# A hand-ordered transformer kernel on one core: key products placed behind the next group's first projection, and small norms placed between attention steps

## The chip, the cores and the metric

The kernel runs on one core of one Trainium2 chip. The metric is the device time of one execution in microseconds (us), taken as the median of several runs.

The engines are named as in the profile: PE is TensorE (matrix products), PEld its weight loads, DVE is VectorE, ACT is ScalarE, POOL is GpSimd and SP is SyncE. Each engine runs its own list of instructions in the order of the program and waits at semaphores for the others.

## The reference, cut to what matters

Two transformer blocks run one after the other on 512 tokens of width 1024, all in float32. The first block is a mixer (a short convolution and differential attention), a cross-attention, and a layer of product-key experts. The second block is a mixer of three parts, a cross-attention and a feed-forward layer with a short convolution.

The change touches two places. The first is how the experts are chosen:

```
q = (hc @ w_pq).reshape(PEER_CHUNK, PEER_HEADS, 2, PEER_DK_HALF)
sc = jnp.einsum('thcd,chnd->thcn', q, sub_keys)        # 128 keys a half
vals, idx = lax.top_k(sc, PEER_TOPK)
cand = vals[:, :, 0, :, None] + vals[:, :, 1, None, :]
top_s, top_c = lax.top_k(cand..., PEER_TOPK)           # 16 experts a head and token
ue, ve = peer_u[experts], peer_v[experts]              # gathered rows
act = gelu(einsum('td,thkd->thk', hc, ue)); out = einsum('thk,thkd->td', g * act, ve)
```

The second is the second block's mixer. Beside the sparse attention (`nsa`) it has a gated part and a convolution part, each with a layer norm, and all three are normed before the output projection:

```
v = layer_norm(v, ln_g, ln_b); mixed = einsum("gts,bcsgd->bctgd", w_s * causal, v) + b_s; y_gmlp = u * mixed
h = causal_depthwise_conv(a * sigmoid(gt), dw_w, dw_b);  y_conv = silu(layer_norm(h, ln_g, ln_b))
y = concat([rms_norm(y_nsa), rms_norm(y_gmlp), rms_norm(y_conv)]);  x = x + y @ w_out
```

## The kernel before, in words

**Halves and tiles.** The 512 tokens are worked on in two halves, `h` = 0 and 1, of 256 tokens, and each half is two tiles of 128 tokens, so that there are four tiles `t`. A projection is cut in chunks. SP loads the chunk's 512 KB of weights into one of six buffers (`RING`), PE multiplies (`proj_T` at L876/L877, `proj_tok` at L896/L897), and the result is copied or combined out of PSUM (`out_T`, `out_tok`) by ACT or DVE.

**One written order.** The class `Plan` writes one list of steps, and each engine follows its own part of that list, in order. Three generators are woven: `work` (the projections and attention of half 1 of block one, then block two of half 0), `choices` (the two rounds of top-16 on DVE, the picking of indices, the softmax of gates) and `peers` (the experts). Each generator has a clock that its steps' costs advance, and the one with the lowest clock goes next. A step that must come after another generator's work yields "wait" until that work is in the list. After the weave, the second block of half 1 (`second(1, False)`) comes alone, and beside it runs `late_down`, the feed-forward output projection of half 0, of which `beside(n)` puts n chunks (L1120; the trace shows a chunk as four instructions of 128x512) between other steps.

**Experts.** For each of 512 experts (128 to a tile) POOL gathers 128 rows of 8 KB (L2125) into one of eight slots, DVE takes a dot product (L1908), ACT applies gelu (L1409), scales it by the gate (L1413, L1416) and, where PE is to add, builds a diagonal matrix (L1421). The sum is made by DVE (L1888) or by PE (L1144/L1145). A slot is free when its sum is done. POOL waits for that.

**Key products.** `scores(h)` runs four groups `c` of four projection chunks `m`. With `lean`, all results leave PSUM on ACT (L1242) into `QH[:, c % 2]`. After a group's fourth chunk is copied out, PE multiplies the group by its keys for both tiles (`scores` on PE, L993), and ACT copies the products out (L1397). DVE's `top` (L1816, L1819, L1824) waits for that copy. `gates` on ACT (L1403) is an exponential, and `gate_sum` on DVE (L1872) waits for it. In half 1 the norm of the second memory follows group 1, and its eight transposes (`trans`, L864/L865, copied out at L1222) follow group 3's products.

**The second block's mixer.** `second(h)` runs twenty steps of `nsa`, a software pipeline over 16 units: PE makes logits (L1088), DVE adds the mask and takes the maximum (L1685), ACT takes exponentials (L1482), DVE weighs them (L1954 to L1969), PE transposes (L1053, L1055), ACT and DVE copy these out (L1500, L2002), and PE multiplies by the values (L1067, L1073). Up to step 15, DVE does four taps of the 31-tap convolution in each step (L1994). After the twenty steps come, in this order:

- `gmlp`: two layer norms on DVE (L2007 to L2023) with a square root on ACT in each (`root`, L1196), PE's gated products (L1096), and DVE's product with u (L2035);
- `conv_out`: PE transposes the convolution (L1105, L1106), two more layer norms, and a silu on ACT (L1519);
- `y_norm`: for each of three parts of `Y`, two squares on ACT (L1191), mean and reciprocal on DVE (L1561, L1563), a square root on ACT (L1196), and then six scalings on DVE (L2054);
- in half 1, the last six chunks of `late_down`, then the transposes of `y` (L864/L865) and the output projection.

**Banks.** The eight PSUM banks are handed out in turn. During the weave six are, since the sums of the experts hold two. A bank is given again when its reader has copied it out.

Of the kernel before, what the change touches and what calls it, by code (L numbers as in the profile page):

```python
# [10 lines left out]
ALU = mybir.AluOpType  # L11
# [91 lines left out]
class Plan:  # L103
# [167 lines left out]
    def scores(self, h, lean):  # L271
        if h == 1:
            self.lent_from = self.last_in.get(7)
        held = None
        for c in range(4):
            for m in range(4):
                k = self.next_ring()
                yield 0, "chunk", "pq", 4 * c + m, k
                if held:
                    yield (0, "out_T") + held  # L280
                yield 3.4, "proj_T", "pq", h, c, m, k
                held = ("pq", h, c, m, lean)
# [4 lines left out]
            if h == 1 and c == 1:  # L287
                yield 0, "mark", ("mem", 2)
                yield from self.norm_steps(("mem", 2), lean)
                self.norming = False  # L290
            if h == 1 and c == 3:
                for i in range(8):
                    yield 0, "trans", ("mem", 2), i, lean
            self.reached.add(("sc", h, c))
# [171 lines left out]
def program(nc, I, out):  # L466
    ctx = ExitStack()
    with ctx:
# [138 lines left out]
        SQ = WKF[:, 0:1024]  # L607

        at = Values()
        ps_of = {}  # L610
# [198 lines left out]
        def tensor_program(e, w):  # L809
# [280 lines left out]
            def gmlp(h):  # L1090
                for c in range(2):
                    ps = bank("gm", h, c)
                    w.wait_ge(*at["ln1", h, c])
                    w.wait_ge(*at["ws"])
                    for g in range(4):
                        mm = e.matmul(ps[:, 64 * g:64 * g + 64], WS[:, g, :], ZG[h][:, c, 256 + 64 * g:320 + 64 * g],  # L1096
                                      start=True, stop=True)
                    mm.then_inc(pe.sem, pe("mm", "gm", h, c))

            def conv_out(h):  # L1100
                for c in range(2):
                    ps = bank("ct", h, c)
                    for m in range(2):
                        w.wait_ge(*at["cv", h, m, 30])
                    e.transpose(ps[:, 0:128], CV[h][:, 0, c * 128:(c + 1) * 128], ident[:, :])  # L1105
                    e.transpose(ps[:, 128:256], CV[h][:, 1, c * 128:(c + 1) * 128], ident[:, :]).then_inc(  # L1106
                        pe.sem, pe("mm", "ct", h, c))
# [71 lines left out]
        def scalar_program(e, w):  # L1179
# [330 lines left out]
            def gmlp(h):  # L1510
                for c in range(2):
                    root(("ln1", h, c), small[:, 407 + 8 * c:408 + 8 * c])

            def conv_out(h):
                for c in range(2):
                    root(("ln2", h, c), small[:, 423 + 8 * c:424 + 8 * c])
                    w.wait_ge(*at["ln2", h, c])
                    d = Y[h][:, c, 768:1024]
                    e.activation(d, d, ACT.Silu).then_inc(act.sem, act("ycv", h, c))  # L1519

            def y_norm(h):
                w.wait_ge(*at["ev", "nv", h, 15])
                w.wait_ge(*at["ev", "gm", h, 1])
                w.wait_ge(*at["ycv", h, 1])
                for q in ENGINES:
                    w.wait_ge(*at["mark", ("y", h), q])
                for j, (a, b) in enumerate(((0, 512), (512, 768), (768, 1024))):
                    squares(("y", h, j), lambda i: Y[h][:, i, a:b], 2, b - a, 448 + 2 * j)
                    root(("y", h, j), small[:, 448 + 2 * j:450 + 2 * j])
# [14 lines left out]
            def hank_in():  # L1544
# [8 lines left out]
                    "nsa": nsa, "gmlp": gmlp, "conv_out": conv_out, "y_norm": y_norm, "mark": marks(act, "act")})  # L1553

        def vector_program(e, w):
# [469 lines left out]
            def gmlp(h):  # L2025
                for c in range(2):
                    v = ZG[h][:, c, 256:512]
                    layer_norm(("ln1", h, c), v, v, "ln1g", "ln1b", 400 + 8 * c, ("ev", "zg", h, 0, 1), ("ln1", h, c))
                for c in range(2):
                    ps = banks[ps_of["gm", h, c]]  # L2030
                    w.wait_ge(*at["mm", "gm", h, c])
                    w.wait_ge(*at["cols"])
                    for g in range(4):
                        sig = ("ev", "gm", h, c) if g == 3 else ("gmp", h, c, g)
                        e.scalar_tensor_tensor(out=Y[h][:, c, 512 + 64 * g:576 + 64 * g], in0=ps[:, 64 * g:64 * g + 64],  # L2035
                                               scalar=col("bs", g), in1=ZG[h][:, c, 64 * g:64 * g + 64], op0=ALU.add,
                                               op1=ALU.mult).then_inc(dve.sem, dve(*sig))

            def conv_out(h):
                for c in range(2):  # L2040
                    layer_norm(("ln2", h, c), banks[ps_of["ct", h, c]][:, 0:256], Y[h][:, c, 768:1024], "ln2g", "ln2b", 416 + 8 * c,
                               ("mm", "ct", h, c), ("ln2", h, c), ("ev", "ct", h, c))

            def y_norm(h):
                parts = ((0, 512), (512, 768), (768, 1024))
                for j, (a, b) in enumerate(parts):
                    inverse(("y", h, j), small[:, 448 + 2 * j:450 + 2 * j], b - a, 1e-6)
                for j in range(3):
                    w.wait_ge(*at["rstd", ("y", h, j)])
                for i in range(2):  # L2050
                    for j, (a, b) in enumerate(parts):
# [19 lines left out]
            def prepare_lambda():  # L2071
                w.wait_ge(*at["rows"])
                for j, (a, b) in enumerate((("lq1", "lk1"), ("lq2", "lk2"))):
# [12 lines left out]
                    "conv_out": conv_out, "y_norm": y_norm, "down": down, "mark": marks(dve, "dve")})  # L2086
# [180 lines left out]
```

## Time and profile before

| what | value |
|---|---|
| median of 3 runs | 2953.93 us (2953.39 to 2955.98) |
| the profiled execution: its time | 2952.47 us |
| its span in the trace | 2950.7 us |
| PE / DVE / ACT / POOL busy | 85% / 60% / 38% / 23% of the span |
| granted PE clock, mean | 0.916 of full speed |
| mean rate of HBM | 284 GB/s |

The profile is of one execution. An engine's share of the span is an average over stages with different limits, so the rows below are read by stretch. The stages of the span, in the order in which the change meets them: the key products of half 0 end near 608 us; those of half 1 run from 1331 to 1434 us; the second block's attention of half 0 runs from about 1672 to 1838 us and its tail to 1879 us; experts go on to 2329 us; the attention of half 1 runs from 2420 to 2553 us and its tail to about 2580 us.

### The profile page before, as it was taken

To read this page: it belongs to the slowest core of one execution; us is meant where nothing else is said; L and a number is where in the kernel's file an instruction comes from. 1 tells how busy PE (TensorE), PEld (TensorE's weight loads), DVE (VectorE), ACT (ScalarE), POOL (GpSimd) and SP (SyncE) were. 2 spreads that over 40 slices of the span, in tenths; PEclk is the share of its full clock that TensorE was granted. 3 is DMA by queue.
4 is the path that set the end of the run, shared out by engine and by line. 5 is a ranking of instruction groups with operands and counts; after the bars stand their busy time and mean duration, and the time that the engine had idled before them with its cause. 6 is when DMAs were issued, how large, how long until landed. Compare 5 with 4: busy or idle time off the path is not lost.

```text
span 2950.7 us, 29550 instructions
## 1 busy us (share of the span) xinstructions
PE 2497.3 (85%) x10118; PEld 1749.2 (59%) x10118; DVE 1760.5 (60%) x4222; ACT 1131.8 (38%) x2759; POOL 681.8 (23%) x566
## 2 busy tenths in 40 slices
PE   8999998889987769779869688587985799888998
PEld 7786665767764337537627544264762476555883
DVE  2101311588697778676879998878998416412430
ACT  2101311242534754454333587464554324412210
POOL 0000000122244334331123445344324101000000
PEclk9999999899998879999989588799997989999999
DMA  6545344689999999999789999899999744432553
GB/s 203 175 153 165 93 143 134 254 302 365 377 400 419 380 405 393 419 368 360 263 337 385 399 372 373 325 419 419 417 418 416 270 155 122 135 130 86 150 154 117
DMA packets 159814, 838.64 MB, mean 284 GB/s; under 512 B 17272, under 2 KB 20744, under 8 KB 93872
## 3 DMA queue, kind: packets, MB, share of 16 engines
q0 software_dynamic: 73728, 536.90, 45.5%
q1 hardware_dynamic: 81312, 287.75, 28.4%
q10 hardware_dynamic: 4624, 12.11, 1.1%
q8 instruction: 80, 1.31, 0.2%
q14 instruction: 70, 0.57, 0.1%
HBM read 828.27 MB, written 8.41 MB: 284 GB/s over the span
## 4 chain that ended last, share of the span: by engine, by line
PE 54%; DVE 18%; ACT 12%; DMA 10%; issue 5%; POOL 1%; DVEq 0%; ACTq 0%; SPq 0%
PE ps L876 25%; DMA BIG<-in_uv,BIG 8%; PE ps L896 5%; PE ps L1120 5%; PE ps L897 5%; DVE X L1888 5%; DVE BIG L1908 5%; PE ps L877 3%; ACT L1409 2%; PE ps L1144 2%; PE ps L1145 2%; DMA BIG<-head_scratch 1%; PE ps L1088 1%; ACT WK L1191 1%; DVE BIG L1819 1%
## 5 line engine op out<-in xcount | busy, mean ns | idle before, releaser
L2125 POOL DMA_INDIRECT BIG<-in_uv,BIG x512 | 639.2, 1249 | 1659.6 <-DVE BIG L1865 556.9
L876 PE MATMUL ps<-BIG,RING 128*128 128x256 f32 x3472 | 807.5, 385 | 16.1 <-DMA RING<-in_w_cq 4.9
L876 PEld LDWEIGHTS ps<-BIG,RING 128*128 128x128 f32 x3472 | 670.0, 194 | 135.3 <-issue 26.4
L1908 DVE CUSTOM_DVE_ANT_0 BIG<-BIG 128x1024 f32<-128x1024 f32 x512 | 620.2, 1220 | 71.0 <-DMA BIG<-in_uv,BIG 68.0
L1888 DVE SCALAR_TENSOR_TENSOR X<-BIG,small,X 128x1024 f32<-128x1024 f32 x333 | 427.6, 1284 | 100.5 <-ACT small L1413 100.2
L1409 ACT ACTIVATE small<-small 128x1 f32<-128x1 f32 x512 | 102.4, 200 | 609.4 <-DVE small L1908 606.3
L876 PE MATMUL ps<-WK,RING 128*128 128x256 f32 x1232 | 289.2, 387 | 24.6 <-DVE BIG L1667 22.6
L876 PEld LDWEIGHTS ps<-WK,RING 128*128 128x128 f32 x1232 | 236.5, 193 | 65.4 <-DVE BIG L1667 30.7
L896 PE MATMUL ps<-RING,BIG 128*128 128x512 f32 (+1 forms) x448 | 225.7, 585 | 7.1 <-DVE BIG L1646 4.4
L897 PE MATMUL ps<-RING,BIG 128*128 128x512 f32 (+1 forms) x448 | 224.1, 582 | 0.0
L1242 ACT ACTIVATE BIG<-ps 128x256 f32<-128x256 f32 (+2 forms) x143 | 56.4, 397 | 402.5 <-PE ps L877 343.0
L1605 DVE TENSOR_SCALAR BIG<-ps 128x256 f32<-128x256 f32 (+2 forms) x37 | 16.8, 454 | 252.1 <-PE ps L877 207.7
L864 PE MATMUL ps<-ident,BIG 128*128 128x128 f32 x128 | 49.6, 396 | 135.2 <-ACT BIG L1213 77.0
L1120 PE MATMUL ps<-RING,BIG 128*128 128x512 f32 x352 | 161.5, 612 | 1.5 <-DVE X L1898 1.5
L1144 PE MATMUL ps<-BIG 128*128 128x512 f32 x178 | 106.3, 682 | 59.6 <-ACT BIG L1421 59.5
L1409 ACT ACT_TABLE_LOAD x119 | 152.7, 1283 | 2.7 <-issue 0.6
L877 PE MATMUL ps<-BIG,RING 128*128 128x256 f32 x496 | 147.5, 379 | 0.0
L896 PEld LDWEIGHTS ps<-RING,BIG 128*128 128x128 f32 x448 | 85.2, 192 | 104.7 <-issue 93.0
L1598 DVE TENSOR_TENSOR X<-ps,X 128x512 f32<-128x512 f32 x40 | 27.4, 690 | 201.0 <-PE ps L897 125.1
L897 PEld LDWEIGHTS ps<-RING,BIG 128*128 128x128 f32 x448 | 85.9, 192 | 102.5 <-issue 101.1
L1144 PE MATMUL ps<-BIG,DG 128*128 128x512 f32 x180 | 111.6, 706 | 34.9 <-ACT DG L1421 34.5
L1191 ACT ACTIVATE WK<-X 128x1024 f32<-128x1024 f32 x32 | 33.8, 1055 | 224.7 <-DVE X L1598 210.6
(255 smaller groups left out, 3143.0 us busy)
## 6 DMA issues: line engine op xcount, KB each, us to landing
RING<-in_w_up SPq DMA_DIRECT2D x88, 512.0 KB
RING<-in_w_down SPq DMA_DIRECT2D x66, 512.0 KB
RING<-in_w_pq SPq DMA_DIRECT2D x32, 512.0 KB
RING<-in_w_cc SPq DMA_DIRECT2D x16, 512.0 KB
RING<-in_w_cx SPq DMA_DIRECT2D x16, 512.0 KB
RING<-in_w_cb SPq DMA_DIRECT2D x16, 512.0 KB
RING<-in_w_cv SPq DMA_DIRECT2D x16, 512.0 KB
RING<-in_w_gc SPq DMA_DIRECT2D x16, 512.0 KB
```

What stands on the lines that cost most here:

```text
L876: e.matmul(ps[:, 0:256], W[:, j, :], src[:, j, 0:256], start=j == 0, stop=False)
L877: e.matmul(ps[:, 0:256], W[:, 7, :], src[:, 7, 0:256], start=False, stop=True).then_inc(pe.sem, pe("mm", site, h, c, m))
L896: e.matmul(ps[:, 0:n], src[:, 2 * j, t * 128:(t + 1) * 128], W[:, 0, :], start=j == 0, stop=False)
L897: mm = e.matmul(ps[:, 0:n], src[:, 2 * j + 1, t * 128:(t + 1) * 128], W[:, 1, :], start=False, stop=j == 3)
L1120: mm = e.matmul(ps[:, :], AF[h][:, f, t * 128:(t + 1) * 128], W[:, hh * 512:(hh + 1) * 512], start=f == 0, stop=f == 21)
L1144: e.matmul(banks[6][:, :], d, v[:, 0:512], start=first, stop=last)
L1145: e.matmul(banks[7][:, :], d, v[:, 512:1024], start=first, stop=last).then_inc(pacc.sem, pacc("sum", k))
L1191: e.activation(SQ[:, 0:width], src(i), ACT.Square, accum_out=small[:, o + i:o + i + 1]).then_inc(act.sem, act("sq", key, i))
L1409: e.activation(a, dots[:, k % 8:k % 8 + 1], ACT.Gelu).then_inc(act.sem, act("gelu", k))
L1888: e.scalar_tensor_tensor(out=X[:, t, :], in0=slot[slot_of[k]][:, 1024:2048], scalar=acts[:, k % 8:k % 8 + 1], in1=X[:, t, :], op0=ALU.mult ...
L1908: e.tensor_tensor_reduce(out=u, in0=HF[:, t % 2, :], in1=u, scale=1.0, scalar=0.0, op0=ALU.mult, op1=ALU.add, accum_out=dots[:, k % 8:k % ...
L2125: e.indirect_dma_start(out=slot[i], out_offset=None, in_=I["uv"], in_offset=bass.IndirectOffsetOnAxis(ap=IDX[:, t, c:c + 1], axis=0)).then ...
```

## The change

**Key products.** A group's last copy out and its products are held back until the first chunk of the next group has been multiplied. Three exceptions stay where they were: group 0 of half 0, and group 3 of both halves, come right behind their own group. In half 1, the second memory's norm goes along with group 1, and its eight transposes come before group 3's products, not behind them.

**Norms.** The functions `gmlp` and `conv_out` are split by the tile index `c`, `gmlp` gets its layer norm as a step of its own (`gmlp_norm`), and these stand behind the attention steps 1 and 2 (norm), 4 and 5 (gated product), and 16 and 17 (convolution's transposes, layer norm and silu). The squares of the gated part and of the convolution part of `Y` stand behind the steps 18 and 19. Of `y_norm` there remain behind the attention: the squares of the attention part, all means and reciprocals (`y_inv`), all three square roots (`y_root`), and the scalings (`y_scale`). In the weave, the three first of these have a cost of 2.6 each, where `gmlp` and `conv_out` had 2.0 each. Those squares write their unused output to `JUNK`, a place of its own. The instructions that the program writes are those of before; none is added or left out. The loads of ACT's function tables are put in when the kernel is built, wherever the function changes.

```
     def scores(self, h, lean):
+        def lists(c):
+            if h == 1 and c == 3:
+                for i in range(8):
+                    yield 0, "trans", ("mem", 2), i, lean
+            for t in range(2):
+                yield 0.9, "scores", h, c, t, lean
+            if h == 1 and c == 1:
+                yield 0, "mark", ("mem", 2)
+                yield from self.norm_steps(("mem", 2), lean)
+                self.norming = False
+            self.reached.add(("sc", h, c))
...
                 yield 3.4, "proj_T", "pq", h, c, m, k
                 held = ("pq", h, c, m, lean)
-            yield (0, "out_T") + held
-            held = None
-            for t in range(2):
-                yield 0.9, "scores", h, c, t, lean
...
+                if m == 0 and c and (h or c > 1):
+                    yield from lists(c - 1)
+            if c == 3 or (h == 0 and c == 0):
+                yield (0, "out_T") + held
+                held = None
+                yield from lists(c)
...
+        gap = 2.6 if lean else 0
+        other = {1: ("gmlp_norm", h, 0), 2: ("gmlp_norm", h, 1), 4: ("gmlp", h, 0), 5: ("gmlp", h, 1),
+                 16: ("conv_out", h, 0), 17: ("conv_out", h, 1), 18: ("y_sq", h, 1), 19: ("y_sq", h, 2)}
         for step in self.phase(True, ((8.0, "nsa", h, i) for i in range(20))):
             self.norming = lean and step[3] >= 18
             yield step
+            if step[3] in other:
+                yield (0,) + other[step[3]]
             yield from beside(1 + step[3] % 2)
-        yield 2.0, "gmlp", h
-        yield 2.0, "conv_out", h
         yield 0, "mark", ("y", h)
-        yield 0, "y_norm", h
+        yield gap, "y_sq", h, 0
+        yield gap, "y_inv", h
+        yield gap, "y_root", h
+        yield 0, "y_scale", h
         yield from beside(7)
...
+            def y_sq(h, j):
+                a, b = Y_PARTS[j]
+                w.wait_ge(*at[(("ev", "nv", h, 15), ("ev", "gm", h, 1), ("ycv", h, 1))[j]])
+                if j == 0:
+                    for q in ENGINES:
+                        w.wait_ge(*at["mark", ("y", h), q])
+                for i in range(2):
+                    own()
+                    e.activation(SQ[:, 0:512] if j == 0 else JUNK, Y[h][:, i, a:b], ACT.Square,
+                                 accum_out=small[:, 448 + 2 * j + i:449 + 2 * j + i]).then_inc(act.sem, act("sq", ("y", h, j), i))
```

## Rows read from the trace of the kernel before

**Rows 1.** Busy time by stretch; columns: stretch, length, PE, PEld, DVE, ACT, POOL busy (instructions), PE clock, DMA share, GB/s.

```profile
560.00:622.00 62.00, 40.14 (x171) 31.51 (x169) 53.52 (x183) 24.97 (x56) 17.88 (x17) 0.84 0.94 368
...
1437.00:1518.00 81.00, 80.41 (x247) 48.22 (x248) 61.54 (x195) 25.94 (x70) 20.08 (x19) 0.98 0.85 317
...
1680.00:1836.00 156.00, 130.69 (x420) 70.69 (x420) 144.27 (x477) 123.47 (x356) 76.73 (x56) 0.85 0.96 377
1836.00:1882.00 46.00, 12.05 (x52) 9.68 (x51) 33.82 (x75) 25.11 (x57) 12.32 (x11) 0.59 0.71 282
...
1912.00:2320.00 408.00, 311.31 (x1128) 218.71 (x1128) 341.91 (x557) 211.50 (x492) 153.14 (x128) 0.90 1.01 418
...
2422.00:2553.00 131.00, 130.96 (x591) 83.99 (x590) 73.64 (x353) 58.19 (x161) 23.02 (x16) 0.95 0.38 112
```

**Rows 2.** Timeline, one full-clock projection chunk to the next (start, length, what).

```profile
1337.28 3.19 PE L876 MATMUL ps<-BIG,RING 128*128 128x256 f32 x14
...
1340.73 3.18 PE L876 MATMUL ps<-BIG,RING 128*128 128x256 f32 x14
```

**Rows 3.** Timeline of half 0's group 2: PE, ACT and DVE (idle before it in brackets).

```profile
584.23 3.75 PE L993 MATMUL ps<-WK,BIG 128*128 128x128 f32 x16 [9.06 <-ACT BIG L1242]
...
588.02 0.60 ACT L1397 ACTIVATE BIG<-ps 128x512 f32<-128x512 f32 x1 [1.11 <-PE ps L993]
...
589.93 0.23 ACT L1403 ACTIVATE BIG<-BIG 128x32 f32<-128x32 f32 x1
...
590.19 0.19 DVE L1872 TENSOR_REDUCE small<-BIG 128x2 f32<-128x32 f32 x1 [4.82 <-ACT BIG L1403]
```

**Rows 4.** Timeline of half 1's groups 0, 2 and 3 on PE and DVE.

```profile
1352.79 0.49 DVE L1816 MAX8 BIG<-BIG 128x8 f32<-128x128 f32 x2 [8.60 <-ACT BIG L1397]
...
1406.11 3.75 PE L993 MATMUL ps<-WK,BIG 128*128 128x128 f32 x16 [7.44 <-ACT BIG L1242]
...
1410.36 0.19 DVE L1872 TENSOR_REDUCE small<-BIG 128x2 f32<-128x32 f32 x1 [2.69 <-ACT BIG L1403]
...
1437.60 4.95 PE L876 MATMUL ps<-BIG,RING 128*128 128x256 f32 x14 [1.95 <-ACT BIG L1222]
```

**Rows 5.** Timeline, half 0's tail: the first two norms, the transposes of y.

```profile
1848.12 0.42 DVE L2007 BATCH_NORM_STATS2 small<-BIG 128x6 f32<-128x256 f32 x1
...
1850.67 0.42 DVE L2007 BATCH_NORM_STATS2 small<-BIG 128x6 f32<-128x256 f32 x1
...
1875.42 0.45 PE L864 MATMUL ps<-ident,BIG 128*128 128x128 f32 x1 [19.25 <-DVE BIG L2054]
```

**Rows 6.** Who waited on DVE, 1848 to 1882 us (total, times, longest).

```profile
DVE small L1561 <- ACT WK L1191: 4.9, 3, 2.2
...
DVE BIG L2015 <- ACT small L1196: 1.9, 4, 1.1
DVE BIG L2035 <- PE ps L1096: 1.3, 1, 1.3
```

**Rows 7.** Timeline of DVE and ACT at half 0's attention step 16.

```profile
1818.17 1.20 DVE L1908 CUSTOM_DVE_ANT_0 BIG<-BIG 128x1024 f32<-128x1024 f32 x1
...
...
1820.77 1.28 ACT L1409 ACT_TABLE_LOAD   x1
1822.06 0.20 ACT L1409 ACTIVATE small<-small 128x1 f32<-128x1 f32 x1
```

**Rows 8.** Timeline of half 1's tail.

```profile
2556.09 1.14 PEld L1096 LDWEIGHTS ps<-BIG,WS 128*128 128x128 f32 x8 [0.39 <-DVE BIG L2023]
...
2558.64 1.10 PE L1096 MATMUL ps<-BIG,WS 128*128 128x64 f32 x8 [1.27 <-DVE BIG L2023]
...
2560.03 10.46 PE L1120 MATMUL ps<-RING,BIG 128*128 128x512 f32 x24
...
2575.85 0.45 PE L864 MATMUL ps<-ident,BIG 128*128 128x128 f32 x1 [5.36 <-DVE BIG L2054]
```

**Rows 9.** Who waited on DVE, 2405 to 2560 us.

```profile
DVE BIG L2002 <- PE ps L1055: 24.7, 13, 6.4
```

More of the change, by code:

```diff
@@ L607, in program @@
         SQ = WKF[:, 0:1024]
+        JUNK = at_(K0 + 4632, 256)
+        Y_PARTS = ((0, 512), (512, 768), (768, 1024))
         at = Values()
@@ L1088, in nsa, with gmlp, conv_out @@
                         e.matmul(ps[:, 0:nn], q, K, start=True, stop=True).then_inc(pe.sem, pe("mm", "nl", h, u, j))
[L1090 to L1107, printed above, removed]
+            def gmlp(h, c):
+                ps = bank("gm", h, c)
+                w.wait_ge(*at["ln1", h, c])
+                w.wait_ge(*at["ws"])
+                for g in range(4):
+                    mm = e.matmul(ps[:, 64 * g:64 * g + 64], WS[:, g, :], ZG[h][:, c, 256 + 64 * g:320 + 64 * g],
+                                  start=True, stop=True)
+                mm.then_inc(pe.sem, pe("mm", "gm", h, c))
+            def conv_out(h, c):
+                ps = bank("ct", h, c)
+                for m in range(2):
+                    w.wait_ge(*at["cv", h, m, 30])
+                e.transpose(ps[:, 0:128], CV[h][:, 0, c * 128:(c + 1) * 128], ident[:, :])
+                e.transpose(ps[:, 128:256], CV[h][:, 1, c * 128:(c + 1) * 128], ident[:, :]).then_inc(
+                    pe.sem, pe("mm", "ct", h, c))
             def down(h, f, k, tiles):
@@ L1508, in nsa, with gmlp_norm, conv_out, y_root @@
                         act.sem, act("ev", "nv", h, u))
[L1510 to L1528, printed above, removed]
+            def gmlp_norm(h, c):
+                root(("ln1", h, c), small[:, 407 + 8 * c:408 + 8 * c])
+            def conv_out(h, c):
+                root(("ln2", h, c), small[:, 423 + 8 * c:424 + 8 * c])
+                w.wait_ge(*at["ln2", h, c])
+                d = Y[h][:, c, 768:1024]
+                e.activation(d, d, ACT.Silu).then_inc(act.sem, act("ycv", h, c))
+            def y_sq(h, j):
[8 more added lines that the diff above has]
+                                 accum_out=small[:, 448 + 2 * j + i:449 + 2 * j + i]).then_inc(act.sem, act("sq", ("y", h, j), i))
+            def y_root(h):
+                for j in range(3):
                     root(("y", h, j), small[:, 448 + 2 * j:450 + 2 * j])
@@ L2023, in layer_norm @@
                 e.tensor_tensor(dst, dst, row(b, key[1]), ALU.add).then_inc(dve.sem, dve(*fin))
[L2025 to L2046, printed above, removed]
+            def gmlp_norm(h, c):
+                v = ZG[h][:, c, 256:512]
+                layer_norm(("ln1", h, c), v, v, "ln1g", "ln1b", 400 + 8 * c, ("ev", "zg", h, 0, 1), ("ln1", h, c))
@@ new lines, in gmlp @@
+            def gmlp(h, c):
+                ps = banks[ps_of["gm", h, c]]
+                w.wait_ge(*at["mm", "gm", h, c])
+                w.wait_ge(*at["cols"])
+                for g in range(4):
+                    sig = ("ev", "gm", h, c) if g == 3 else ("gmp", h, c, g)
+                    e.scalar_tensor_tensor(out=Y[h][:, c, 512 + 64 * g:576 + 64 * g], in0=ps[:, 64 * g:64 * g + 64],
+                                           scalar=col("bs", g), in1=ZG[h][:, c, 64 * g:64 * g + 64], op0=ALU.add,
+                                           op1=ALU.mult).then_inc(dve.sem, dve(*sig))
@@ L2050, in y_norm @@
                 for i in range(2):
-                    for j, (a, b) in enumerate(parts):
+                    for j, (a, b) in enumerate(Y_PARTS):
                         o = 448 + 2 * j + i
```

18 lines of the change are left out of this document (8 added, 10 removed).

## The prediction

> **What bounds the kernel now.** I read the page first: PE is busy for 85% of the span, but the chain that ended last is shared between PE, DVE, ACT and gathers, so no one engine is the bound and each place must be read by itself. I then read the busy time by stretch, the timelines of the places that the change touches, and who waited for whom there.
>
> Four kinds of stretch follow one another [rows 1]. Where half 0's key products run (560 to 622 us), DVE is busy for 53.52 of 62 us and PE for 40.14: DVE and its waits set the pace. From 1437 to 1518 us PE is busy for 80.41 of 81 us. From 1680 to 1836 us, half 0's attention beside the experts, DVE is busy for 144.27 of 156 us. From 1912 to 2320 us the DMA share is 1.01: the gathers are the bound, and projections of half 0 made sooner there end nothing sooner; only experts that have come further by 1912 do. From 2422 to 2553 us, half 1's attention, PE is busy for 130.96 of 131 us.
>
> All lists are written in one order, so a time saved where an engine sets the pace moves everything behind it forward, unless another bound has covered it.
>
> **Key products, half 0.** Groups 0 and 3 stay. Group 1 moves past one projection chunk, 3.45 us from start to start [rows 2]. DVE waits for its first gather then, and I cost this edit at nothing; without that cover it would be up to 3.45 us. Group 2 is the one that counts. Its products waited 9.06 us for a copy out that ACT made only after an expert's gelu, and began at 584.23. ACT copied both results out, the second at 588.02, and only then made the exponential (589.93), for which DVE's gate sum had waited 4.82 us at 590.19 [rows 3]. With the products one chunk later in the list, `gates` falls ahead of them (the products' 3.4 of clock against 0.9), so ACT makes its 1.28 us table load and 0.23 us exponential right behind the copy out, by about 585.7. DVE then needs group 2's first result. PE has the next chunk behind it already and can begin the products at 584.2 as before: half of 3.75 us and a 0.60 us copy give 586.8. Before, DVE reached that work at 590.19 and its three small instructions, 590.7. So 3.9 us are saved on DVE, which sets the pace. Bounds: nothing, and the idle time with the chunk gained, 4.82 us.
>
> **Key products, half 1.** Here group 0 moves too, and DVE stood idle for 8.60 us until 1352.79 for just that result [rows 4]. It comes at least 3.45 us later. An expert's dot product (1.20 us [rows 7]) or two will be listed ahead of it in that hole, so DVE lags by 1 to 3 us. At group 2, PE's 7.44 us of idle time holds the next chunk, and DVE's wait of 2.69 us for the exponential goes as in half 0. I count half of these 2.69 us, 1.3, as what is left after the lag. At group 3 the memory's transposes come first, so that their copies lie beside the products: the 1.95 us that the next projection waited go, and its first chunk, 4.95 us at 1437.60 because PE's clock had fallen in the pauses, should take the 3.19 us of [rows 2], 1.8 us less. These 3.7 us are saved on PE, which is full from there to 1518 [rows 1]. The exponential of `gates` comes behind the eight copies now, so DVE waits there somewhat longer; DVE has 19 us of idle time in the 81 that follow, which hide it. In all 5.0 us. Bounds: a loss of 1 us, if the lag of 3 stays and PE must wait for experts' gates; a gain of 7.2 us, 3.7 and the whole chunk of 3.45.
>
> **Norms, half 0.** Nothing is taken out; work moves from the tail into an attention in which DVE is nearly full. Each of four layer norms costs DVE 2.55 us (1848.12 to 1850.67 [rows 5]). What can be gained is idle time. In the tail DVE waited 4.9 us for squares, 1.9 us for roots and 1.3 us for PE [rows 6], 8.1 us in all. With the squares ahead and the rest beside experts these go. In exchange, DVE now stands at each root behind ACT's exponentials. Read at step 16: DVE ends the step's own work about 1818.2 and needs some 0.9 us up to the reciprocal, but ACT is free only at 1820.77 and then has a load of 1.28 us and a root of 0.20 us, 1822.25 [rows 7]: a wait of 3.1 us. Queued behind it on DVE are the dot products, and for these ACT's gelu, PE's sums and POOL's free slots. I take 3.1 us for this worst step and half, 1.5 us, for each of the three others, 7.7 us. Net: a gain of 0.4 us. Bounds: a gain of 8.1 us if the 12 us in which DVE is idle in 1680 to 1836 take these waits, and a loss of 8 us if they are twice as long. The moved matrix products, transposes and silus cost the same and lie where PE is no bound. POOL and SP issue nothing new; the output projection's weights are asked for behind the same chunks.
>
> ACT goes from one table to the next with 0.01 us between the load's end and the gelu (1820.77, 1.28, 1822.06) [rows 7]. The Trainium skill ("ScalarE: Activation LUTs", What ACT_TABLE_LOAD costs) states a drain of about 1.38 us beside each load, 2.66 us a switch, and advises to group functions by table, which speaks against roots between exponentials. By that rule each of the four waits would be 1.38 us longer and the sum 5.5 us higher, about 2943 us; by the row it stays. The trace shows the load's length as stated and no drain.
>
> **Norms, half 1.** PE is the bound, and it waited 0.39 and 1.27 us for the gated products and 5.36 us for the normed y, 7.0 us together [rows 8]. DVE waited 24.7 us at one place of the pipeline alone for PE [rows 9] and is busy 73.64 of 131 us, so four norms of 2.55 us, and a wait for PE's gated product at steps 4 and 5, are hidden by PE's attention and feed-forward chunks; without that cover it would be 10 us. What is late next is the y norm itself: it can begin when the last attention result is out, near 2553, and needs two squares, six small instructions, a load of 1.28 us, three roots of 0.20 us [rows 7] and six scalings; I estimate some 7 us, half of it the squares and scalings (eight passes over at most 512 elements, at about the 0.42 us of 256 elements in [rows 5]), so it is done near 2560. PE then still has its six chunks, 10.46 us [rows 8], so nothing is late. A gain of 7.0 us, bounds 5 and 7.3.
>
> **The sum.** -3.9 - 5.0 - 0.4 - 7.0 = -16.3 us. The profiled execution took 2952.47 us (span 2950.7), so 2936.2 us; it lies 1.5 us under the median of 2953.93, so the forecast for a median is 2937.6, rounded to 2938 us. The order in the weave shifts by an expert or so at each moved step, which I can't cost; I allow 4 us to either side.
>
> **The rivals.**
> 1. The key products bring nothing (chance 0.20). The lag of half 1's first top-16 and the later results eat what the chunk gives. For it: the 8.60 us hole ends exactly with that result. Against: the 4.82 us wait. The norms alone give 7.4 us: 2946.5 us.
> 2. Half 0's norms are hidden after all (0.13). DMA's share is 0.71 from 1836 to 1882 against 1.01 later, 14 us of gathering not done [rows 1]. If the moved norms fall into time in which DVE waits for gathers anyway, the 8.1 us are a full gain: 2930 us.
> 3. The change doesn't do what it says in half 1's tail (0.10): the y norm's chain is stretched by DVE's leftovers of step 17 or by bank order, so that PE still waits about 5 us, and half 0 loses 4 us: 2947 or, with rival 1 as well, 2953 us, no change.
> 4. Slower (0.07): half 0's attention takes the DVE work and the tail gives nothing back, because the gathers were the bound there too. Four norms at their work of 2.55, 1.7 us of gated products and four waits of 3.1 us make 24 us against 15.9 gained elsewhere: 2962 us. It decides against the change when the waits pass 2.5 us each and nothing is refunded. For it: the DMA share of 0.96 in the attention. Against: the 14 us of idle DMA.
>
> **How the numbers follow.** My forecast has a chance of 0.50, with a range of its own from 2932 to 2943. Eight times in ten I expect 2926 to 2952, which takes in rivals 1 and 2 and the better part of 3. A measurement here can tell about 0.2%, 5.9 us. Faster by more than that, under 2948: forecast, rivals 1 and 2, less their edges, 0.77. Within it: most of rival 3 and edges, 0.15. Slower: rival 4 and part of 3, 0.08.
>
> **What would show it.** Half 0's group 2: DVE's wait at L1872 of 4.82 us under 1 us. Half 1: the products of group 0 one chunk later, DVE's hole longer; at group 3 no 1.95 us wait ahead of the next projection and its first chunk near 3.2 us. Half 0: waits of DVE at L2015 of 1 to 3 us in steps 1, 2, 16 and 17, a DMA share above 0.71 after the attention, and about as many experts done at the same time. Half 1: no idle PE ahead of L1096, and L864 right behind the last L1120. The prediction is wrong if DVE's added waits in half 0 are far from 8 us, if experts' order shifts by more than one or two at a step, or if PE's clock falls in a stretch where it was full.

## The result and the profile after

The changed kernel took 2939.4 us in the median of 6 runs (2936.01 to 2945.88), beside 2954.82 us of the kernel before (6 runs). The ratio is 0.9949, 95% interval [0.9933, 0.9965]: 15.1 us less, where 16.3 us less had been forecast. In a second series beside the other experiments the ratio was 0.9955 [0.9943, 0.9967], 13.3 us less. Two of the 29 executions of the kernel before in that series took 3711 and 3816 us at a granted clock of 0.66 and 0.64, and no ratio counts them. The profiled execution took 2945.88 us, with a span of 2944.2 us. It is the slowest of its six, so I use the second series' traced execution as well (2936.95 us, span 2935.2); "the first trace" and "the second trace" of the changed kernel below are these two.

The kernel's line numbers have moved: PE's L864 is now L880, L876 L892, L993 L1009, L1096 L1111, L1120 L1134; ACT's L1196 is L1210, L1397 L1411, L1403 L1417; DVE's L1872 is L1889, L1908 L1925, L1888 L1905, L1898 L1915, L2015 L2032, L2054 L2071.

Busy time by stretch, the changed kernel (columns as in [rows 1]):

```profile
560.00:622.00 62.00, 43.52 (x194) 34.67 (x194) 54.70 (x186) 25.85 (x60) 20.88 (x19) 0.86 0.98 387
1437.00:1518.00 81.00, 76.48 (x240) 45.21 (x238) 67.89 (x206) 26.77 (x69) 23.27 (x20) 0.99 0.93 352
1680.00:1836.00 156.00, 120.28 (x386) 65.33 (x387) 140.42 (x468) 120.28 (x337) 68.06 (x49) 0.84 0.89 351
1836.00:1882.00 46.00, 16.78 (x76) 11.08 (x74) 40.17 (x80) 28.88 (x77) 23.61 (x17) 0.70 0.98 379
...
1912.00:2320.00 408.00, 311.62 (x1128) 220.72 (x1128) 343.73 (x557) 211.99 (x492) 152.59 (x127) 0.90 1.01 415
2422.00:2553.00 131.00, 128.81 (x581) 82.55 (x580) 83.19 (x386) 70.84 (x175) 23.03 (x16) 0.95 0.37 111
```

In half 0 the gathers lost 0.07 of the DMA time in the attention (156 us) and won 0.27 of it in the 46 us of the tail: 10.9 us against 12.4 us. That is the exchange of which the forecast spoke. From 1912 to 2320 us the DMA share is 1.01 as before.

Timeline of half 0's group 2 in the changed kernel, against [rows 3]:

```profile
587.28 3.76 PE L1009 MATMUL ps<-WK,BIG 128*128 128x128 f32 x16 [6.57 <-ACT BIG L1256]
591.16 0.58 ACT L1411 ACTIVATE BIG<-ps 128x512 f32<-128x512 f32 x1
591.75 1.28 ACT L1417 ACT_TABLE_LOAD   x1
593.05 0.23 ACT L1417 ACTIVATE BIG<-BIG 128x32 f32<-128x32 f32 x1
593.31 0.19 DVE L1889 TENSOR_REDUCE small<-BIG 128x2 f32<-128x32 f32 x1
```

DVE's gate sum has no wait in brackets any more (it was 4.82 us). The exponential stands between the two copies out, not ahead of the first as I had read the list. Two smaller waits of the gate sum behind it, which the prediction had not read, are gone as well. In the kernel before they were:

```profile
616.10 0.19 DVE L1872 TENSOR_REDUCE small<-BIG 128x2 f32<-128x32 f32 x1 [1.07 <-ACT BIG L1403]
...
643.29 0.19 DVE L1872 TENSOR_REDUCE small<-BIG 128x2 f32<-128x32 f32 x1 [1.93 <-ACT BIG L1403]
```

The three waits were 7.8 us together.

Half 1's group 3 on PE, against [rows 4]:

```profile
1430.57 0.27 PE L880 MATMUL ps<-ident,BIG 128*128 128x128 f32 x1
...
1432.32 1.14 PE L1009 MATMUL ps<-WK,BIG 128*128 128x128 f32 x8
1433.30 1.02 PE L1158 MATMUL ps<-BIG 128*128 128x512 f32 x2
...
1435.01 1.05 PE L1009 MATMUL ps<-WK,BIG 128*128 128x128 f32 x8
1435.90 3.19 PE L892 MATMUL ps<-BIG,RING 128*128 128x256 f32 x14
```

The next projection has no wait, and its first chunk takes 3.19 us where it took 4.95. PE's wait of 1.28 us among the transposes is gone too. In the kernel before it was:

```profile
1434.84 0.33 PE L864 MATMUL ps<-ident,BIG 128*128 128x128 f32 x1 [1.28 <-ACT BIG L1222]
```

Half 1's tail on PE, against [rows 8]:

```profile
2557.97 0.43 PE L1089 MATMUL ps<-BIG 31*128 31x64 f32 x2
2558.33 14.00 PE L1134 MATMUL ps<-RING,BIG 128*128 128x512 f32 x32
2572.17 0.27 PE L880 MATMUL ps<-ident,BIG 128*128 128x128 f32 x1
```

L880 comes right behind the last chunk. Its transposes take 0.27 us each and not 0.45. In the kernel before, PE had stood idle for 5.36 us, and the clock granted to the transposes behind that was 0.50 of full speed, the lower of the two levels (1.2 GHz):

```profile
2575.80:2580.00 4.20, 3.93 (x16) 3.00 (x16) 2.74 (x6) 2.00 (x5) 0.00 (x0) 0.50 0.00 0
```

In the changed kernel it was 1.00, the upper level (2.4 GHz), from 2572.2 to 2575 us.

The y norm itself was done later than forecast. The last attention result came at 2558.4 us and not near 2553, ACT's first squares of the attention part waited until 2562.07, and DVE's scalings ended at 2567.3 where the forecast had said "near 2560". PE's last chunk ended at 2572.3, so the norm stayed hidden, with some 5 us to spare.

Who waited on DVE from 1640 to 1885 us in the changed kernel (total, times, longest), against [rows 6]:

```profile
DVE X L1905 <- ACT small L1427: 6.5, 10, 2.1
DVE BIG L2032 <- ACT small L1210: 6.4, 4, 1.6
DVE BIG L2052 <- PE ps L1111: 3.7, 1, 3.7
```

The four waits for a root are 6.4 us together; 7.7 us had been forecast. Each of them is 1.60 us. The third, with what ACT did during it:

```profile
1838.19 1.28 ACT L1210 ACT_TABLE_LOAD   x1
1839.48 0.20 ACT L1210 ACTIVATE small<-small 128x1 f32<-128x1 f32 x1
...
1839.72 0.54 DVE L2032 TENSOR_SCALAR BIG<-ps,small 128x256 f32<-128x256 f32 x1 [1.60 <-ACT small L1210]
```

All but some 0.1 us of the wait is the table load and the root. ACT had nothing else in hand: at none of the four did DVE stand behind exponentials, as the forecast had it.

The experts' progress shows how such a gain travels. Expert n is the n-th dot product of DVE (L1908 before, L1925 after; first rows of each here), and the table gives its start less that of the kernel before, in us. A plus is a lag, a minus a lead. A run's own offset at expert 0 is chance and may be taken off the whole column. One trace is one execution: five kernels whose list of steps is that of the kernel before up to the 144th expert lie there 0.1 to 3.7 us behind it with their offset taken off.

```profile
562.97 1.23 DVE L1908 CUSTOM_DVE_ANT_0 BIG<-BIG 128x1024 f32<-128x1024 f32 x1 [1.69 <-DMA BIG<-in_uv,BIG]
...
645.24 1.22 DVE L1908 CUSTOM_DVE_ANT_0 BIG<-BIG 128x1024 f32<-128x1024 f32 x1
```

```profile
565.33 1.23 DVE L1925 CUSTOM_DVE_ANT_0 BIG<-BIG 128x1024 f32<-128x1024 f32 x1 [4.67 <-DMA BIG<-in_uv,BIG]
...
640.78 1.22 DVE L1925 CUSTOM_DVE_ANT_0 BIG<-BIG 128x1024 f32<-128x1024 f32 x1
```

| expert (before at) | changed | changed, 2nd | order set back | half 0's keys alone | half 1's keys alone | all but half 0's keys | changed, sums on DVE |
|---|---|---|---|---|---|---|---|
| 0 (563.0) | +2.4 | +0.9 | -0.2 | +1.8 | +2.8 | +0.9 | -0.2 |
| 16 (645.2) | -4.5 | -5.9 | -7.0 | -5.1 | +2.8 | +1.0 | -7.0 |
| 32 (715.3) | -0.7 | -2.3 | -3.4 | -1.3 | +2.8 | +1.0 | -3.3 |
| 144 (1075.1) | +10.9 | +8.0 | +1.7 | +3.5 | +4.9 | +3.9 | +7.7 |
| 208 (1294.2) | +4.6 | +0.7 | +2.9 | -5.0 | +5.8 | +4.2 | +1.5 |
| 256 (1522.5) | -5.2 | -10.2 | -4.7 | +3.0 | -3.4 | -5.1 | -13.8 |
| 352 (1819.3) | +12.1 | +6.9 | +9.9 | +4.6 | -1.6 | +11.6 | +6.0 |
| 368 (1885.0) | -5.2 | -10.4 | -7.3 | +3.9 | -1.9 | -5.6 | -11.3 |
| 511 (2322.8) | -2.3 | -8.4 | -5.7 | +5.6 | +0.3 | -2.5 | -9.4 |

### The profile page after: what moved, and what is told of

Its sections match the earlier page's. It is cut to its first block, busy times and chain, and to the rows that moved or that the text cites. A ratio compares the mean times of both kernels' runs of the same rounds, so it can differ in the third digit from the quotient of the medians.

```text
span 2944.2 us, 29556 instructions
## 1 busy us (share of the span) xinstructions
PE 2499.7 (85%) x10118; PEld 1751.4 (59%) x10118; DVE 1760.1 (60%) x4222; ACT 1134.4 (39%) x2762; POOL 676.5 (23%) x566
## 4 chain that ended last, share of the span: by engine, by line
PE 57%; DVE 18%; ACT 11%; DMA 10%; issue 4%; POOL 0%; ACTq 0%; DVEq 0%; SPq 0%
PE ps L892 26%; DMA BIG<-in_uv,BIG 7%; PE ps L912 6%; PE ps L913 6%; PE ps L1134 5%; DVE BIG L1925 5%; DVE X L1905 4%; PE ps L893 4%; PE ps L1158 2%; PE ps L1159 2%; ACT L1423 2%; DMA BIG<-head_scratch 2%; DVE BIG L1836 1%; DVE BIG L1833 1%; PE ps L1104 1%
## 5 line engine op out<-in xcount | busy, mean ns | idle before, releaser
L892 PE MATMUL ps<-BIG,RING 128*128 128x256 f32 x3472 | 808.1, 385 | 13.8 <-DMA RING<-in_w_cq 4.9
L892 PEld LDWEIGHTS ps<-BIG,RING 128*128 128x128 f32 x3472 | 670.4, 194 | 133.7 <-issue 28.6
L1925 DVE CUSTOM_DVE_ANT_0 BIG<-BIG 128x1024 f32<-128x1024 f32 x512 | 619.4, 1218 | 73.0 <-DMA BIG<-in_uv,BIG 70.3
L1905 DVE SCALAR_TENSOR_TENSOR X<-BIG,small,X 128x1024 f32<-128x1024 f32 x333 | 426.9, 1282 | 108.7 <-ACT small L1427 106.7
L892 PE MATMUL ps<-WK,RING 128*128 128x256 f32 x1232 | 290.8, 389 | 21.7 <-DVE BIG L1684 19.9
L892 PEld LDWEIGHTS ps<-WK,RING 128*128 128x128 f32 x1232 | 238.6, 195 | 62.4 <-DVE BIG L1684 27.0
L912 PE MATMUL ps<-RING,BIG 128*128 128x512 f32 (+1 forms) x448 | 223.0, 579 | 5.1 <-DVE BIG L1663 2.4
L1134 PE MATMUL ps<-RING,BIG 128*128 128x512 f32 x352 | 161.9, 614 | 1.5 <-DVE X L1915 1.5
L1158 PE MATMUL ps<-BIG,DG 128*128 128x512 f32 x180 | 110.2, 698 | 61.3 <-ACT DG L1435 61.2
L880 PE MATMUL ps<-ident,BIG 128*128 128x128 f32 x128 | 48.0, 387 | 131.2 <-ACT BIG L1227 76.1
L912 PEld LDWEIGHTS ps<-RING,BIG 128*128 128x128 f32 x448 | 84.4, 190 | 102.1 <-issue 92.8
L1158 PE MATMUL ps<-BIG 128*128 128x512 f32 x178 | 109.2, 699 | 34.2 <-ACT BIG L1435 34.1
```

What stands on the lines that cost most here:

```text
L892: e.matmul(ps[:, 0:256], W[:, j, :], src[:, j, 0:256], start=j == 0, stop=False)
L912: e.matmul(ps[:, 0:n], src[:, 2 * j, t * 128:(t + 1) * 128], W[:, 0, :], start=j == 0, stop=False)
L1134: mm = e.matmul(ps[:, :], AF[h][:, f, t * 128:(t + 1) * 128], W[:, hh * 512:(hh + 1) * 512], start=f == 0, stop=f == 21)
L1158: e.matmul(banks[6][:, :], d, v[:, 0:512], start=first, stop=last)
L1905: e.scalar_tensor_tensor(out=X[:, t, :], in0=slot[slot_of[k]][:, 1024:2048], scalar=acts[:, k % 8:k % 8 + 1], in1=X[:, t, :], op0=ALU.mult ...
L1925: e.tensor_tensor_reduce(out=u, in0=HF[:, t % 2, :], in1=u, scale=1.0, scalar=0.0, op0=ALU.mult, op1=ALU.add, accum_out=dots[:, k % 8:k % ...
```

## The experiments

All ratios are to the kernel before on the same chip, and 0.001 is 2.95 us; kernels of different series are compared by these ratios, with both intervals. Parts that were "not moved" are written as in the kernel before.

**The two halves of the change, and a repetition.** The first kernel leaves the norms behind the attention (`gmlp_all`, `conv_all` and `y_norm` are the old steps, both tiles or all three parts at once):

```
         for step in self.phase(True, ((8.0, "nsa", h, i) for i in range(20))):
...
-            if step[3] in other:
-                yield (0,) + other[step[3]]
...
+        yield 2.0, "gmlp_all", h
+        yield 2.0, "conv_all", h
         yield 0, "mark", ("y", h)
-        yield gap, "y_sq", h, 0
-        yield gap, "y_inv", h
-        yield gap, "y_root", h
-        yield 0, "y_scale", h
+        yield 0, "y_norm", h
```

> Only the placing of the key products is changed; the norms stay behind the attention. My theory: a gain of 3.9 us in half 0 (group 2's exponential no longer behind the products) and 5.0 us in half 1 (group 3's transposes ahead of its products, one projection chunk inside PE's wait), so 8.9 us less than the kernel before, a ratio near 0.997. Rival 1, the key products bring nothing: 0 us, ratio 1.000. A third reading, that the traced run of the changed kernel suggests: the experts were up to 10.9 us behind between 1026 and 1140 us in it; if this comes from the new order of steps and not from that one execution, it is here again in the trace.

Measured: 0.9978 [0.9969, 0.9988], 6.5 us less. Rival 1 (the key products bring nothing) falls. The lag at the 144th expert was there again (+7.8 us), so it isn't the chance of one execution alone.

The second leaves the key products where they were (the loop of `scores` as before):

```
+                yield (0, "out_T") + held
+                held = None
+                for t in range(2):
+                    yield 0.9, "scores", h, c, t, lean
...
-                if m == 0 and c and (h or c > 1):
-                    yield from lists(c - 1)
```

> Only the norms are moved, in both halves; the key products stay. My theory: a gain of 0.4 us in half 0 and 7.0 us in half 1, 7.4 us in all, a ratio near 0.9975. If half 0's waits at the roots are not given back in the tail, slower than that by up to 8 us, so no gain; if they are hidden entirely, 15 us faster.

Measured: 0.9975 [0.9962, 0.9988], 7.4 us less, as forecast.

The third moves the norms in half 1 alone:

```
-            if step[3] in other:
+            if h == 1 and step[3] in other:
```

> Only the norms of half 1 are moved. My theory: 7.0 us less than the kernel before, a ratio near 0.9976, by the three waits of PE in the tail (0.39, 1.27 and 5.36 us) alone; the trace of the changed kernel shows 1.9 us of warm instead of cold transposes on top and some 2 us of new waits of PE in the attention. Rival 3, no gain in the tail: 0 us. The difference to the run in which both halves are moved is half 0's part: 0.4 us by my theory, 8 us either way by its bounds.

Measured: 0.9978 [0.9969, 0.9987], 6.5 us less. Half 0's norms are the difference to the kernel above, 0.9 us with an uncertainty of some 5 us: neither a gain of 8 us nor a loss of 8 us.

The fourth is the changed kernel again.

> The changed kernel itself once more, beside the others on one chip. The ratio should be near the 0.995 measured. If the experts' lag of 10.9 us near 1080 us belongs to the order of the steps, its new trace shows it again; if it was that one execution, it does not, and the span is shorter than 2944 us by several us.

Measured: 0.9955 [0.9943, 0.9967]; the lag was there (+8.0), and the span was 9.0 us shorter all the same.

**The key products by half, and the changed kernel without half 0's norms.** Half 0 alone has the new placing for h = 0 only, half 1 alone for h = 1 only (the loop of before under a condition on h).

> Only half 0's key products are placed anew (groups 1 and 2 one projection chunk later). My prediction's term: 3.9 us faster than the kernel before. The traces so far say otherwise: the experts are 7 us ahead at the 16th (645 us), 2 us ahead at the 64th to 112th, and 8 us behind at the 144th, because the shifted clock makes DVE meet the sum in another place of the differential attention's steps (9 us more of waiting for the scaled gate between 960 and 1090 us). By that: 1 us slower to 2 us faster, ratio 0.9995 to 1.0005, with the lag at the 144th expert in the trace.

Measured: 1.0022 [1.0011, 1.0033], 6.5 us more. Both theories missed it. On its own this part makes the kernel slower. The lead of the first 16 experts is there (-5.1 us). The lag that I expected at the 144th is not: +3.5 us, of which +1.8 is the offset, although the list of steps is the changed kernel's, step for step, up to the 220th expert. What the trace shows is later: 2.3 us ahead at the 255th expert, 3.0 us behind at the 256th. Between these two DVE stood at the total of tile 1, behind a sum that PE had behind chunks of the value projection (DVE's waits, 1460 to 1530 us, this kernel; then the kernel before):

```profile
DVE X L1964 <- PE ps L1195: 12.3, 1, 12.3
```

```profile
DVE X L1898 <- PE ps L1145: 1.2, 1, 1.2
```

In this kernel PE sums 11 of the last 16 experts of tile 1, among them the last, and in the kernel before ten, the last one by DVE. PE is full here from 1460 to 1520 us:

```profile
1460.00:1520.00 60.00, 60.00 (x173) 32.67 (x172) 40.13 (x128) 19.95 (x53) 16.31 (x15) 1.00 0.94 354
```

> Only half 1's key products are placed anew (all groups, and group 3's transposes first). My prediction's term: 5.0 us faster. If half 0's placing is worth nothing in the end, this one carries all of the 6.5 us that both gave (ratio 0.9978), and the trace shows no lag at the 144th expert. Rival: both are needed, and this one alone gives 3 us or less.

Measured: 0.9982 [0.9972, 0.9993], 5.3 us less; 5.0 had been the term. At the 144th expert, up to which its list is that of the kernel before, it stands at +4.9 against +2.8 at expert 0.

> The changed kernel, but half 0's norms stay behind its attention. My theory: half 0's norms are worth 0.4 us, so this is as fast as the changed kernel (ratio 0.9955). If half 0's move gave a gain of 8 us, this is 8 us slower than the changed kernel; if it cost one, it is faster: 2930 us.

Measured: 0.995 [0.9937, 0.9963], within the noise the same as the changed kernel. Half 0's norms are worth nothing that can be measured here either.

**Is the lag at the 144th expert worth time?** In half 1's differential attention each step lasts 9.0 on the work's clock and an expert 3.1, so three experts fall between two steps, and one of three is summed by DVE. So the same order comes back step after step. In the kernel before, from step 6 to 14, the expert that DVE sums is the second of the three and its sum comes last: three dot products of DVE stand between the step's own work and the sum. In the changed kernel, from step 3 to 12, that expert is the first, and only two dot products stand ahead of its sum, where DVE waits longer for the gate that ACT scales.

```
-        yield 0, "mark", ("da", h)
+        yield -2.5 * h, "mark", ("da", h)
```

> The changed kernel with the clock of the work generator set back by 2.5 at the start of half 1's differential attention, so that from step 5 to 14 the summed expert comes in the middle of three and the sum last, as in the kernel before (there from step 6 to 14; in the changed kernel only from step 14). No instruction is added. If the order of these steps makes the lag, the experts are some 8 to 10 us earlier at the 144th than in the changed kernel. In the time: a gain of up to 8 us if nothing behind it sets the pace, and 0 us if it is the lag that the kernel makes up by the 208th expert anyway; I expect 2 us faster than the changed kernel, ratio 0.995.

Measured: 0.9965 [0.9952, 0.9979]. DVE's wait for the scaled gate from 960 to 1090 us (total, times, longest) in the changed kernel, then in this one:

```profile
DVE X L1905 <- ACT small L1427: 37.8, 14, 6.0
```

```profile
DVE X L1905 <- ACT small L1427: 29.8, 13, 6.2
```

The 144th expert is at +1.7 instead of +10.9 and +8.0. Seven traces have the changed kernel's order in this stretch. With their offsets taken off, six of them lag by 6.2 to 8.6 us, with waits of 36.9 to 37.8 us, and one does not, that of half 0's keys alone (1.7 us):

```profile
DVE X L1954 <- ACT small L1463: 30.9, 14, 5.8
```

The kernel before and the five with its order wait 27.2 to 30.8 us. So the order makes the lag in most executions and not in every one; what decides was not found. And the kernel is not faster without it: the changed one makes the lag up by the 224th expert (-1.1 us), where half 1's key products on PE are waited for anyway. The total of tile 1 too had only 1.2 us of wait here, and that brought nothing visible either.

**The end of tile 1.** Here the last eight experts of tile 1 are summed by DVE, first with half 0's key products alone, then in the changed kernel:

```
-                    if n % 3 if self.light else n % 2:
+                    if (n % 3 if self.light else n % 2) and (t != 1 or c < 120):
```

> Half 0's key products alone, as in the run that was slower (1.0022), and the sums of the last eight experts of tile 1 on DVE, none of them on PE. In that slower run DVE waited 12.3 us at the total of tile 1 for a sum that PE had behind eight chunks of the value projection. My theory: this wait is what made it slower; without it the kernel is 3 to 6 us faster than that run, ratio 0.9998 to 1.001. Rival: PE is full there and sets the pace itself, then only the PE time of some five sums (1.7 us each) goes, and the ratio stays at 1.0015 or above.

Measured: 0.9997 [0.9988, 1.0006], 7.4 us less than the run at 1.0022 (by the two intervals 3 to 12 us less): the slowness is gone. Here six sums went from PE to DVE. The total is not waited for any more, and the kernel stands at the 256th expert at -0.6 us, 3.5 us ahead of the kernel before when the offset of +2.9 is taken off.

> The changed kernel with the same edit: the last eight experts of tile 1 are summed by DVE. It waited 8.6 to 10.8 us at that total in the two traces of the changed kernel, against 1.2 us before. By the theory of the wait: 3 to 6 us faster than the changed kernel, ratio 0.993 to 0.994. If PE sets the pace: 2 us or less, ratio 0.9945 or above.

Measured: 0.9912 [0.9896, 0.9928], 26 us less than the kernel before and 11 to 13 us less than the changed one, by the intervals anything from 4 to 19 us. It is faster than both theories had it. Five sums went from a full PE to a DVE that waited (1437 to 1518 us, second trace of the changed kernel, then this one; the total of tile 1 in the first trace of the changed kernel, then here):

```profile
1437.00:1518.00 81.00, 74.81 (x225) 42.70 (x223) 68.16 (x216) 28.09 (x74) 22.67 (x20) 0.96 0.94 354
```

```profile
1437.00:1518.00 81.00, 68.72 (x212) 40.17 (x210) 79.06 (x231) 31.07 (x78) 25.50 (x22) 0.93 0.96 369
```

```profile
1513.59 1.29 DVE L1915 TENSOR_TENSOR X<-ps,X 128x512 f32<-128x512 f32 x2 [10.82 <-PE ps L1159]
```

```profile
1504.92 1.29 DVE L1915 TENSOR_TENSOR X<-ps,X 128x512 f32<-128x512 f32 x2
```

Five sums of 1.72 us each (two instructions of L1158 and two of L1159) are 8.6 us of PE, and PE is busy for 6.1 and 7.8 us less than in the two traces of the changed kernel. I had called "PE sets the pace" a rival worth 2 us or less, and that size was wrong: if PE is the bound, its 8.6 us are the gain. This edit takes away both the wait and PE's work; the kernel with the order set back had only the wait taken away and won nothing. That speaks for PE's work, but the two were not separated in one pair of kernels, and the trace does not show the gain. It is of the slowest of only four executions (2924.08 to 2936.06 us), and with 2936.06 us as long as the changed kernel's second trace (2936.95). With the offsets taken off it is 2.5 us ahead of that trace at the 256th expert and level with it at the 511th. Where the 11 to 13 us of the untraced executions come from is open.

**Group 3's transposes alone**, in the kernel before:

```
+                if h == 1 and c == 3:
+                    for i in range(8):
+                        yield 0, "trans", ("mem", 2), i, lean
                 for t in range(2):
                     yield 0.9, "scores", h, c, t, lean
```

> The kernel before with one thing changed: in half 1 the eight transposes of the second memory come before group 3's products. My prediction's term for this alone: 3.7 us faster (1.95 us of PE's wait and 1.8 us of cold first chunk), ratio 0.9987. If it is 0, half 1's 5 us come from the products placed one chunk later.

Measured: 0.9984 [0.9971, 0.9997], 4.7 us less. The lists of the two kernels differ in nothing but this, so it is the cleanest pair here. It accounts for most of the 5.3 us of half 1's key products, as far as intervals of some 4 us can tell.

**All but half 0's key products.**

> The changed kernel, but half 0's key products stay where they were in the kernel before. By my prediction's term it loses 3.9 us against the changed kernel (ratio 0.9965). By the runs of the key products so far (half 1 alone 0.9982, both 0.9978, half 0 alone 1.0022) half 0's placing is worth nothing here or less: ratio 0.9935 to 0.9955.

Measured: 0.9967 [0.9955, 0.9979], 3.5 to 5.3 us more than the two series of the changed kernel. That is near my prediction's term of 3.9 us, and outside what I expected after the runs of the key products. But the interval of this ratio overlaps with both of the changed kernel's, which are of other series, so the sign of the term in the whole change is likely and not shown.

## Why the prediction came out

| step | forecast | measured |
|---|---|---|
| key products, half 0 | -3.9 | +6.5 alone; -1.2 on top of half 1's; -3.5 to -5.3 in the whole change |
| key products, half 1 | -5.0 | -5.3 (transposes first: -4.7) |
| norms, half 0 | -0.4 | -0.9; and -0.3 to +1.5 in the whole change |
| norms, half 1 | -7.0 | -6.5 |
| sum | -16.3 | -15.1 and -13.3 |

The figures of each half's key products alone, of the transposes, of half 1's norms and of the sum are ratios to the kernel before, and their intervals leave out zero. The others are differences of two ratios, uncertain by some 4 to 5 us each, and show no sign for certain. Half 0's and half 1's key products alone add up to +1.2 us, and together they gave -6.5 us: these parts do not add.

**Key products, half 0.** The wait of 4.82 us went as foreseen, and the local gain was larger than 3.9 us: 6.8 us at the 16th expert (-4.46 less +2.36; 6.7 to 6.8 in all eight traces with this placing). The two further waits of the gate sum that went, 1.07 and 1.93 us, are most of the surplus. 3.8 us were given back by the 32nd expert, 2.4 of them where DVE waited 8.8 us for PE at L1634 and before 6.4 at L1617, so that some 3 us were left. What I did not cost was the rest of the list. The sentence "the order in the weave shifts by an expert or so at each moved step, which I can't cost; I allow 4 us to either side" was the weak step: 4 us was too little for this part, which alone came out 10.4 us from its term. The shifted order moved DVE's sums against the attention's steps (6 to 9 us of lag in most traces, made up later) and the end of tile 1, where an edit of the list was worth 7.4 us in one kernel and 11 to 13 in another. That the sum came out so well is in part luck: such shifts cancelled in the whole change, and the run of this part alone shows that they need not.

**Key products, half 1.** Right in place for group 3, and near in size (3.7 us forecast, 4.7 measured), though a wait of 1.28 us among the transposes went that the sum had left out. The "hole" of group 0 was to grow by a chunk; in the changed kernel it was 4.57 us instead of 8.60, with the experts placed differently ahead of it, while with half 0's placing left out it was 10.7 us. The 1.3 us for group 2 was not separated by any run.

**Norms, half 0.** The exchange was there as forecast: 6.4 us of waits at the roots, 12 us of lag at the 352nd expert, all given back by the 368th. The cause of the waits was read wrongly. The forecast took 3.1 us at step 16, for ACT busy with the step's exponentials, and half of that, by guess, at the three others; each wait was 1.60 us, ACT's table load and root alone. That 7.7 came near 6.4 is luck. I had not foreseen the 3.7 us that DVE waited for PE's gated product. Rivals 2 and 4 (all hidden; nothing refunded) both fall, by the two pairs of kernels with and without half 0's norms; the term of 0.4 us itself is far below what these pairs can tell. ACT's tables behaved as the row ahead of the prediction said (changed kernel, half 1's step 16):

```profile
2542.63 1.28 ACT L1210 ACT_TABLE_LOAD   x1
2543.92 0.20 ACT L1210 ACTIVATE small<-small 128x1 f32<-128x1 f32 x1
2544.14 1.28 ACT L1531 ACT_TABLE_LOAD   x1
```

Root and load follow each other with 0.01 to 0.02 us between them. The Trainium skill ("ScalarE: Activation LUTs", What ACT_TABLE_LOAD costs) gives the load's 1.28 us, which the trace shows, and a drain of about 1.38 us, which it does not.

**Norms, half 1.** The tail's three waits went, and the transposes ran at the upper clock level (some 1.9 us that I had not counted: 5.6 us of lead at the first L912 against 3.7 at L880). Against this stand small new waits of PE for DVE in the attention (0.98 us the longest in the first trace), costed at nothing, and in some executions the clock, below. Rival 3 falls: the three waits were gone, and half 1's norms alone gave 6.5 us. The y norm's chain was indeed 7 us later than I had worked out, and only the chunks behind the attention hid it.

## What to carry to other kernels

Where one written order is woven from streams with clocks, moving a step is two changes: the one in place, which a timeline prices well, and a shift of everything behind it. Test each moved part alone and together, and look at orders that come back step after step and at the ends of tiles, where one engine's sum is read behind another's queue. Beside a full PE, giving five sums to DVE measured more here (11 to 13 us, 4 to 19 by the intervals) than the placing of any step; why it was so much was not shown.

## What the runs showed of the hardware that was not expected

PE's granted clock fell in the middle of half 1's attention in some executions. Rows of 2450 to 2480 us: the changed kernel's first trace, its second, and the kernel with only half 1's norms moved.

```profile
2450.00:2480.00 30.00, 29.51 (x134) 19.86 (x133) 19.50 (x101) 13.11 (x41) 5.76 (x5) 0.89 0.30 95
```

```profile
2450.00:2480.00 30.00, 30.00 (x142) 19.62 (x142) 19.19 (x93) 13.45 (x40) 5.13 (x4) 1.00 0.33 106
```

```profile
2450.00:2480.00 30.00, 29.50 (x132) 19.71 (x131) 18.75 (x93) 13.30 (x41) 6.14 (x5) 0.89 0.35 104
```

In the first trace PE had waited 0.98 us at 2438.79 and 0.36 us at 2452.42, and from 2454.26 a group of six L1104 took 2.35 us instead of 1.69 and a group of eight L1134 5.48 us instead of 3.70:

```profile
2454.26 2.35 PE L1104 MATMUL ps<-BIG 64*128 64x384 f32 x6
2456.55 1.97 PE L1111 MATMUL ps<-BIG,WS 128*128 128x64 f32 x8
2458.31 5.48 PE L1134 MATMUL ps<-RING,BIG 128*128 128x512 f32 x8
```

That is 3.3 us, with the 0.87 us of L1111 (1.10 us at full clock). The granted clock in the middle of it was 0.50, the lower level (1.2 GHz), and PE was busy throughout:

```profile
2457.00:2461.00 4.00, 4.00 (x12) 2.45 (x12) 2.31 (x14) 0.62 (x1) 0.71 (x1) 0.50 0.01 2
```

The same list ran at full clock in the second trace. The row of 2450 to 2480 us is 0.89 in three of the eight traces whose half 1 has its norms moved, and 1.00 in all six without. It can be one part of the spread of 10 us among executions of one kernel. The small waits alone do not decide it. All eight traces with the norms moved have two of them here, of 0.18 to 1.26 us and of 0.36 to 0.37 us. The three whose clock fell had 0.89 to 1.09 us at the first, and two that stayed at 1.00 had 1.25 and 1.26 us. What does decide it is open.
